# Moving a norm factor out of the linear operand of a gated feed-forward and giving its unit high and low activations in one 512-column matmul

## The chip, the cores and the metric

The kernel runs on one core of a Trainium2 chip. The metric is device time in microseconds (us) of the whole program, the median over executions. Inputs and outputs are float32.

## What is computed

Two transformer-like blocks on 256 tokens of width 1024: attention, feed-forward, a spatial gating unit, feed-forward again, then a state-space and attention mixer and an MLP. Every sub-block takes a normed input and its output is normed before it is added to the residual. The change touches the two feed-forwards:

```python
def rms_norm(x, g):
    y = xf * lax.rsqrt(jnp.mean(xf * xf, axis=-1, keepdims=True) + EPS)
    return y * g

def conv_gated_ffn(h, w_in, conv_w, conv_b, w_out):      # D_FF = 2816
    g, u = jnp.split(h @ w_in, 2, axis=-1)
    gp = jnp.pad(g, ((0, 0), (CONV_WIDTH - 1, 0), (0, 0)))
    g = conv_b + sum(conv_w[k] * gp[:, k:k + S] for k in range(CONV_WIDTH))
    return (jax.nn.gelu(g) * u) @ w_out

h = conv_gated_ffn(rms_norm(x, norm_ffn_pre[i]), ...)
x = x + rms_norm(h, norm_ffn_post[i])
```

Here g is the gated operand (it goes through the convolution and the gelu) and u is the linear one. The factor r of the norm in front belongs to a token, so it can be taken out of `h @ w_in`; u enters the output linearly, so r of u can be taken through `w_out` too, up to the following norm.

## The kernel before

All weights come in units of 128 x 1024 floats (512 KB) through a ring of six: SP loads `raw` (L2052), ScalarE rounds it to `w_hi` (`hi_of`, L151), VectorE computes the remainder `w_lo` (`lo_of`, L156). Activations are held as `a_hi` and `a_lo` in the same way, and a product of full precision is three matmuls, hi x hi, hi x lo and lo x hi (`three`, L172 to L175). A slot of the ring is free for rounding again when TensorE has used the unit (`unit_used`), and free for loading when `lo_done` says so.

**A feed-forward** has 22 tiles of 128 hidden features. For tile t TensorE runs (`ffn_in_pe`, L501) one unit for g and one for u, each `features` (L178): 8 slices of the width by three matmuls, with 256 moving columns (the tokens), 24 matmuls per unit. Two tiles behind, it runs `accumulate` (L205) for the output: 12 matmuls of 512 columns with one unit of `w_out` and the finished activations of tile t - 2. Tiles 0 to 3 are written out, tiles 4 to 19 are a hardware loop of two tiles per turn (`Fori`, with semaphore values and column addresses computed in registers), tiles 20 and 21 are written out again. The last four output units are held back (`held_pe`, L322) and run by token tile, first all four for token tile 0, then for token tile 1, so that the norm behind can begin. PSUM banks alternate by the parity of t (`f_banks`), so TensorE waits before the g unit of tile t until tile t - 2 has left its banks (L503).

Per tile **VectorE** runs, in its program's order (`ffn_dve_step`, L563): g times the row of norm factors `ROW` into `pad` (L572), the three taps of the convolution (L576, L580 twice), `w_lo` of two units ahead (the two calls of `split`), the product of gated and linear operand `F_PR` (L586), its remainder `a_lo` (L589), and a third `w_lo`. **ScalarE** (`ffn_act_step`, L534) runs: a `w_hi`, the gelu (L540), a `w_hi`, the rounding of `F_PR` to `a_hi` (L545), a `w_hi`. **GpSimd** (`ffn_pool_step`, L548) multiplies the gelu's result by `ROW` (L553). ScalarE waits for the convolution before the gelu and for `product` before the rounding; VectorE waits for `w_hi` before each `w_lo`, for GpSimd before the product and for `a_hi` before the remainder. What lies behind a waiting instruction of an engine waits with it.

**Between the sub-blocks** stands an `update` (L429 to L468): squares of the result for its norm (L368), the root (L376), the term `acc * row` (`term_dve`, L408), the reciprocal (L414), the addition to x (L418), transposition and rounding for the next sub-block, the factor of the next norm (L426). There are six updates; updates 1 and 3 follow the feed-forwards. `row_pe` and `row_dve` turn the factors of the norm before a feed-forward into `ROW` by two small matmuls and a copy.

Of the kernel before, what the change touches and what calls it, by code (L numbers as in the profile page):

```python
# [8 lines left out]
F32R = mybir.dt.float32r  # L9
# [77 lines left out]
def build(nc, w, x_in, cols_in, misc_in, tables_in, rows_in, ws_in, wdt_in, out):  # L87
    def sb(name, shape, dt=F32):
        return nc.alloc_sbuf_tensor(name, shape, dt)
# [11 lines left out]
    x = sb("x", [P, TT, D])  # L101


    a_hi = sb("a_hi", [P, 2 * KT, SEQ], F32R)
    a_lo = sb("a_lo", [P, 2 * KT, SEQ], F32R)
    cols = sb("cols", [P, COLS])
    misc = sb("misc", [P, MISC])
    tab = sb("tab", [P, TABLES])
# [69 lines left out]
    def features(pe, n, o, i=0, pre=None):  # L178
# [45 lines left out]

    Norm = namedtuple("Norm", "n sum mean root inv scaled turned hi lo")
    Pre = namedtuple("Pre", "lo base")
    Update = namedtuple("Update", "n n_last part base term sum root inv added next")

    ROW = cut(16384, SEQ)
    EPS_COL = st[:, 90:91]  # L230
# [70 lines left out]
                                     ALU.subtract).then_inc(q.lo, 1)  # L301


    def update(n, n_last):
        return Update(n, n_last, *post_sems, next_sems)

    acc = [ps[:, 2 * tt:2 * tt + 2, :].rearrange("p a b -> p (a b)") for tt in range(TT)]

# [62 lines left out]
    def root_act(act, u, tt):  # L371
        if tt:
            act.wait_ge(u.base, u.n + 1)
        act.wait_ge(u.sum, 3 * u.n + 2 * tt + 1)
        k = 23 if tt else 20
        act.activation(st[:, 4 + tt:5 + tt], st[:, k:k + 1], ACT.Sqrt, bias=st[:, 24:25] if tt else EPS_COL,  # L376
                       scale=1.0 / D).then_inc(u.root, 1)

    def next_act(act, u, tt):
        act.wait_ge(u.added, 4 * u.n + 2 * tt + 2)  # L380
# [19 lines left out]
    def term_dve(dve, u, tt, h, r):  # L400

        acc_ready(dve, u, tt, h)
        dve.wait_ge(u.sum, 3 * u.n + (h + 2 if tt else 1))
        if tt and h == 0:
            dve.tensor_scalar(st[:, 24:25], st[:, 22:23], 1.0 / D, EPS, ALU.mult, ALU.add).then_inc(u.base, 1)
        if tt == 0:
            dve.wait_ge(row_loaded[r % 2], 16 * (r // 2 + 1))
        dve.tensor_tensor(ybuf[:, tt, half(h)], acc[tt][:, half(h)], row[:, r % 2, half(h)],  # L408
                          ALU.mult).then_inc(u.term, 1)

    def add_dve(dve, u, tt):

# [8 lines left out]
    def half(h):  # L421
        return slice(h * D // 2, (h + 1) * D // 2)
# [60 lines left out]
            add_dve(dve, u, tt)  # L483


    F_CV, F_GL, F_PR, F_GR = cut(3072, 2, SEQ), cut(3584, 2, SEQ), cut(4096, 2, SEQ), cut(4608, 2, SEQ)

    def ffn_sems(name):
        return signals(name, "copied conv gelu scaled product hi lo")

    def f_g(n0, t):
        return n0 + (2 * t if t < 2 else 3 * t - 2 if t < FT - 1 else 3 * t - 3)
# [19 lines left out]
    def ffn_pe(pe, f, n0, u, following, turn_early=True):  # L512
        features(pe, n0, ps[:, 0, 0:SEQ], pre=after(u))
        row_pe(pe, u, 1)
        features(pe, n0 + 1, ps[:, 3, 0:SEQ])
        ffn_in_pe(pe, f, n0, 1)
        ffn_in_pe(pe, f, n0, 2)
        pe.wait_ge(next_sems.row_out, f_row[f])
        pe.wait_ge(f.lo, 1)
        accumulate(pe, f_out(n0, 0), f_slot(0), True, False)  # L520
        ffn_in_pe(pe, f, n0, 3)
        pe.wait_ge(f.lo, 2)
        accumulate(pe, f_out(n0, 1), f_slot(1), False, False)
# [31 lines left out]
    def ffn_pool(pool, f):  # L555
        pool.wait_ge(next_sems.row_out, f_row[f])
        for t in range(2):
            ffn_pool_step(pool, f, t)
        with pool.Fori(0, (FT - 2) // 2) as i:
            for t in (2, 3):  # L560
                ffn_pool_step(pool, f, t, i)
# [1479 lines left out]
    with nc.Block() as block:  # L2041
# [18 lines left out]
        def _(pool):  # L2060
# [71 lines left out]
        def _(dve):  # L2132
# [176 lines left out]
```

## Time and profile before

| | us |
|---|---|
| median of 3 runs | 1118.3 (1117.46 to 1119.08) |
| the profiled execution, device time | 1117.81 |
| its span, first to last instruction | 1116.0 |
| first feed-forward, first `pad` to last `a_lo` starting | 111.2 to 281.9 |
| second feed-forward, the same | 528.5 to 699.1 |

The profile names engines PE (TensorE matmul), PEld (its weight load), DVE (VectorE), ACT (ScalarE), POOL (GpSimd). Times of the timeline are from the start of the span. Matmuls are pipelined, so the distance from one start to the next is what one costs, not its own duration.

### The profile page before, as it was taken

What the parts mean: (1) busy time and instruction counts of PE and PEld (TensorE: products, weight loads), DVE (VectorE), ACT (ScalarE), POOL (GpSimd) and SP (SyncE); (2) the same over time, 40 slices, a digit from 0 to 9 for tenths busy, and PEclk for the clock granted to TensorE, in tenths of its full rate; (3) what the DMA queues carried; (4) which work ended last, traced back from release to release, by engine and by line L of the source; (5) the groups of instructions that cost most, each with busy time, mean ns of one, the idle gap of its engine ahead of it and who ended that gap; (6) DMA issues with size and microseconds to landing.
All of it is one profiled execution on the core that took longest, in us unless ns stands there. A gap on an engine that the chain in (4) does not pass through costs nothing.

```text
span 1116.0 us, 20509 instructions
## 1 busy us (share of the span) xinstructions
PE 1077.4 (97%) x7130; PEld 964.4 (86%) x7130; DVE 782.0 (70%) x1330; ACT 631.1 (57%) x1126; POOL 96.8 (9%) x119
## 2 busy tenths in 40 slices
PE   7989999999999999999999999999998998999998
PEld 7978999999788998788999999899576877999997
DVE  6657877777754457886877777798678748666664
ACT  6657444444755856666444444777767646444443
POOL 0140111111010002220111111000000000000000
PEclk9999999999999999999999999999999999999999
DMA  8353656555366374442655555364111544555541
GB/s 328 111 196 120 221 188 199 195 184 193 118 245 200 120 232 161 150 161 86 219 184 198 188 191 186 103 205 166 57 57 58 167 154 148 191 188 188 188 150 38
DMA packets 51381, 185.07 MB, mean 166 GB/s; under 512 B 5728, under 2 KB 6240, under 8 KB 51328
## 3 DMA queue, kind: packets, MB, share of 16 engines
q1 hardware_dynamic: 49248, 178.28, 48.2%
q0 software_dynamic: 1504, 5.44, 1.4%
q8 instruction: 34, 0.56, 0.2%
q10 hardware_dynamic: 576, 0.64, 0.2%
q14 instruction: 19, 0.16, 0.0%
HBM read 183.29 MB, written 1.05 MB: 165 GB/s over the span
## 4 chain that ended last, share of the span: by engine, by line
PE 88%; DVE 6%; ACT 3%; issue 2%; DMA 1%; DVEq 0%; SPq 0%; ACTq 0%
PE ps L215 28%; PE ps L173 18%; PE ps L175 18%; PE ps L174 18%; DVE w_lo L156 2%; PE ps L1559 1%; PE ps L675 1%; DVE a_lo L396 1%; ACT a_hi L390 1%; PE ps L704 1%; PE ps L688 1%; DVE arena L771 1%; PE ps L1570 1%; PE ps L939 1%; DMA x<-in_x 1%
## 5 line engine op out<-in xcount | busy, mean ns | idle before, releaser
L156 DVE TENSOR_TENSOR w_lo<-raw,w_hi 128x1024 fp32r<-128x1024 f32 x336 | 418.0, 1253 | 135.6 <-ACT w_hi L151 135.5
L151 ACT ACTIVATE w_hi<-raw 128x1024 fp32r<-128x1024 f32 x336 | 347.3, 1052 | 158.7 <-PE ps L175 100.1
L173 PE MATMUL ps<-a_hi,w_hi 128*128 128x256 f32 x1408 | 400.0, 284 | 2.2 <-DVE a_lo L396 1.4
L175 PE MATMUL ps<-a_hi,w_lo 128*128 128x256 f32 x1408 | 398.4, 283 | 0.0
L174 PE MATMUL ps<-a_lo,w_hi 128*128 128x256 f32 x1408 | 398.3, 283 | 0.0
L173 PEld LDWEIGHTS ps<-a_hi,w_hi 128*128 128x128 f32 x1408 | 269.8, 192 | 7.7 <-issue 3.6
L174 PEld LDWEIGHTS ps<-a_lo,w_hi 128*128 128x128 f32 x1408 | 269.9, 192 | 2.6
L175 PEld LDWEIGHTS ps<-a_hi,w_lo 128*128 128x128 f32 x1408 | 269.9, 192 | 0.0
L215 PE MATMUL ps<-w_hi,a_hi 128*128 128x512 f32 x496 | 162.4, 401 | 7.8 <-DVE a_lo L1144 2.8
L215 PE MATMUL ps<-w_lo,a_hi 128*128 128x512 f32 x496 | 157.7, 391 | 0.0
L215 PE MATMUL ps<-w_hi,a_lo 128*128 128x512 f32 x496 | 157.3, 390 | 0.0
L215 PEld LDWEIGHTS ps<-w_lo,a_hi 128*128 128x128 f32 x496 | 93.1, 188 | 20.5
L215 PEld LDWEIGHTS ps<-w_hi,a_lo 128*128 128x128 f32 x496 | 93.1, 188 | 20.5
L215 PEld LDWEIGHTS ps<-w_hi,a_hi 128*128 128x128 f32 x496 | 85.8, 189 | 23.8 <-issue 3.9
L540 ACT ACTIVATE arena<-arena 128x256 f32<-128x256 f32 x44 | 18.4, 418 | 101.4 <-DVE arena L580 101.4
L553 POOL TENSOR_TENSOR arena<-arena 128x256 f32<-128x256 f32 x44 | 47.1, 1071 | 309.8 <-ACT arena L540 309.8
L545 ACT ACTIVATE a_hi<-arena 128x256 fp32r<-128x256 f32 x44 | 18.4, 418 | 77.8 <-DVE arena L586 76.1
L173 PE MATMUL ps<-w_hi,a_hi 128*128 128x512 f32 (+1 forms) x160 | 61.2, 383 | 0.6 <-DVE a_lo L396 0.6
L175 PE MATMUL ps<-w_hi,a_lo 128*128 128x512 f32 (+1 forms) x160 | 59.0, 369 | 0.0
L174 PE MATMUL ps<-w_lo,a_hi 128*128 128x512 f32 (+1 forms) x160 | 59.0, 368 | 0.0
L580 DVE SCALAR_TENSOR_TENSOR arena<-pad,cols,arena 128x256 f32<-128x256 f32 x88 | 42.7, 485 | 10.2 <-DVE arena L576 0.3
L173 PEld LDWEIGHTS ps<-w_hi,a_hi 128*128 128x128 f32 x160 | 30.2, 188 | 7.7 <-issue 2.7
(193 smaller groups left out, 1007.9 us busy)
## 6 DMA issues: line engine op xcount, KB each, us to landing
raw<-in_w SPq DMA_DIRECT2D x336, 512.0 KB, 3.4
row<-in_rows POOLq DMA_DIRECT2D x7, 512.0 KB, 4.2
x<-in_x SPq DMA_DIRECT2D x2, 512.0 KB, 5.0
out<-x SPq DMA_DIRECT2D x4, 256.0 KB, 2.0
misc<-in_misc POOLq DMA_DIRECT2D x1, 512.0 KB, 5.6
arena<-in_ws POOLq DMA_DIRECT2D x1, 512.0 KB, 7.1
tab<-in_tables POOLq DMA_DIRECT2D x1, 320.0 KB, 4.4
tab<-in_tables POOLq DMA_DIRECT2D x1, 256.0 KB, 4.7
```

The costliest lines, as they stand in the source:

```text
L151: act.activation(w_hi[:, s, :], raw[:, s, :], ACT.Copy).then_inc(hi_done, 1)
L156: dve.tensor_tensor(w_lo[:, s, :], raw[:, s, :], w_hi[:, s, :].bitcast(F32), ALU.subtract).then_inc(lo_done, 1)
L173: pe.matmul(o, l_hi, r_hi, start=first, stop=False)
L174: pe.matmul(o, l_hi, r_lo, start=False, stop=False)
L175: return pe.matmul(o, l_lo, r_hi, start=False, stop=last)
L215: mm = pe.matmul(ps[:, 2 * tt + c, :], a[:, slot, t], b[:, s, c * 512:(c + 1) * 512], start=f, stop=z)
L390: act.activation(a_hi[:, k, tile(tt)], spun(tt, k), ACT.Copy, scale=gain(g, k)).then_inc(u.next.hi, 1)
L396: dve.scalar_tensor_tensor(a_lo[:, k, tile(tt)], spun(tt, k), gain(g, k), a_hi[:, k, tile(tt)].bitcast(F32), ALU.mult, ALU.subtract).then_ ...
L540: act.activation(F_GL[:, b, :], F_CV[:, b, :], ACT.Gelu_apprx_tanh).then_inc(f.gelu, 1)
L545: act.activation(a_hi[:, f_slot(t), :], F_PR[:, b, :], ACT.Copy).then_inc(f.hi, 1)
L553: pool.tensor_tensor(F_GR[:, b, :], F_GL[:, b, :], ROW, ALU.mult).then_inc(f.scaled, 1)
L580: dve.scalar_tensor_tensor(F_CV[:, b, :], pad[:, b, k:k + SEQ], col(k), F_CV[:, b, :], ALU.mult, ALU.add).then_inc(f.conv, 1)
```

## The change

The operand u is no longer multiplied by the norm factor. The product is gelu(g) times the unnormed u; the output of the feed-forward is then too large by 1/r per token, which updates 1 and 3 put right (`power` 1: the term is multiplied by r, and the mean of squares by r squared). GpSimd's product is gone. The u unit is computed by `features_apart`: `a_hi` and `a_lo` lie in one buffer `both`, and one matmul of 512 columns applies `w_hi` to both, with the results side by side in the bank; a second of 256 columns adds `w_lo` x `a_hi` to the first half. The halves must then be added: ScalarE copies the second half out of PSUM (`F_UP`), VectorE adds it to the first (`F_US`), and then multiplies. TensorE's wait at L503 is for the sum in place of the product. `factors_dve` (two operations of two columns each) stands on VectorE ahead of each feed-forward.

```diff
-    a_hi = sb("a_hi", [P, 2 * KT, SEQ], F32R)
-    a_lo = sb("a_lo", [P, 2 * KT, SEQ], F32R)
+    both = sb("both", [P, 2, 2 * KT, SEQ], F32R)
+    a_hi, a_lo = both[:, 0], both[:, 1]
...
+    def features_apart(pe, n, bank, i=0, pre=None):
+
+        s = n % RING
+        pe.wait_ge(lo_done, n + 1 + RING * i)
+        for k in range(KT):
+            if pre is not None:
+                pe.wait_ge(pre.lo, pre.base + k + 1)
+            c = slice(k * P, (k + 1) * P)
+            pe.matmul(ps[:, bank, :].rearrange("p (h t) -> p h t", h=2), w_hi[:, s, c], both[:, :, k, :],
+                      start=k == 0, stop=False)
+            mm = pe.matmul(ps[:, bank, 0:SEQ], w_lo[:, s, c], a_hi[:, k, :], start=False, stop=k == KT - 1)
+        mm.then_inc(unit_used, 1)
...
+    def factors_dve(dve, u):
+
+        n = sum(v.power > 0 for v in updates[:u.n])
+        dve.wait_ge(u.next.inv, TT * u.n)
+        r, f = st[:, 14:14 + TT], st[:, FACTOR:FACTOR + TT]
+        if u.power == 2:
+            dve.tensor_tensor(f, r, r, ALU.mult).then_inc(factor_ready, 1)
+        else:
+            dve.tensor_copy(f, r).then_inc(factor_ready, 1)
+        dve.wait_ge(factor_ready, 2 * n + 1)
+        dve.scalar_tensor_tensor(st[:, FACTOR_SQ:FACTOR_SQ + TT], f, 1.0 / D, f, ALU.mult,
+                                 ALU.mult).then_inc(factor_ready, 1)
...
-        dve.tensor_tensor(ybuf[:, tt, half(h)], acc[tt][:, half(h)], row[:, r % 2, half(h)],
-                          ALU.mult).then_inc(u.term, 1)
+        if u.power:
+            dve.scalar_tensor_tensor(ybuf[:, tt, half(h)], acc[tt][:, half(h)], factor(u, tt), row[:, r % 2, half(h)],
+                                     ALU.mult, ALU.mult).then_inc(u.term, 1)
...
     def ffn_in_pe(pe, f, n0, t, i=0):
         if t >= 3:
-            pe.wait_ge(f.product, t - 1 + 2 * i)
+            pe.wait_ge(f.summed, t - 1 + 2 * i)
         g_bank, u_bank = f_banks(t, i)
         features(pe, f_g(n0, t), ps[:, g_bank, 0:SEQ], i)
-        features(pe, f_g(n0, t) + 1, ps[:, u_bank, 0:SEQ], i)
+        features_apart(pe, f_g(n0, t) + 1, u_bank, i)
...
         act.wait_ge(f.conv, 3 * t + 3 + 6 * i)
         if t >= 2:
-            act.wait_ge(f.scaled, t - 1 + 2 * i)
+            act.wait_ge(f.product, t - 1 + 2 * i)
         act.activation(F_GL[:, b, :], F_CV[:, b, :], ACT.Gelu_apprx_tanh).then_inc(f.gelu, 1)
         split(1)
+        act.wait_ge(unit_used, f_g(n0, t) + 2 + RING * i)
+        if t >= 2:
+            act.wait_ge(f.summed, t - 1 + 2 * i)
+        act.activation(F_UP[:, b, :], ps[:, f_banks(t, i)[1], SEQ:2 * SEQ], ACT.Copy).then_inc(f.part, 1)
         act.wait_ge(f.product, t + 1 + 2 * i)
...
-    def ffn_pool_step(pool, f, t, i=0):
-        b = t % 2
-        pool.wait_ge(f.gelu, t + 1 + 2 * i)
-        if t >= 2:
-            pool.wait_ge(f.product, t - 1 + 2 * i)
-        pool.tensor_tensor(F_GR[:, b, :], F_GL[:, b, :], ROW, ALU.mult).then_inc(f.scaled, 1)
...
         split(0)
         split(1)
-        dve.wait_ge(f.scaled, t + 1 + 2 * i)
-        dve.wait_ge(unit_used, f_g(n0, t) + 2 + RING * i)
-        dve.tensor_tensor(F_PR[:, b, :], F_GR[:, b, :], ps[:, u_bank, 0:SEQ],
-                          ALU.mult).then_inc(f.product, 1)
+        dve.wait_ge(f.part, t + 1 + 2 * i)
+        dve.tensor_tensor(F_US[:, b, :], F_UP[:, b, :], ps[:, u_bank, 0:SEQ], ALU.add).then_inc(f.summed, 1)
+        dve.wait_ge(f.gelu, t + 1 + 2 * i)
+        dve.wait_ge(f.summed, t + 1 + 2 * i)
+        dve.tensor_tensor(F_PR[:, b, :], F_GL[:, b, :], F_US[:, b, :], ALU.mult).then_inc(f.product, 1)
...
+            factors_dve(dve, updates[1])
             ffn_dve(dve, ffn[0], N_FFN0, 0)
```

## Rows read from the trace of the kernel before

**Rows 1.** The page: the chain that ended last, shares of the span by engine.

```profile
PE 88%; DVE 6%; ACT 3%; issue 2%; DMA 1%; DVEq 0%; SPq 0%; ACTq 0%
```

**Rows 2.** Busy time in a stretch of the first feed-forward's loop (stretch, length, engines).

```profile
138.00:269.00 131.00, 131.00 (x925) 123.40 (x924) 97.78 (x145) 58.57 (x80) 16.73 (x16) 1.00 0.59 192
```

**Rows 3.** Timeline of PE over one tile: start, duration, instruction.

```profile
204.61 0.63 PE L215 MATMUL ps<-w_hi,a_hi 128*128 128x512 f32 x2
...
207.36 0.28 PE L173 MATMUL ps<-a_hi,w_hi 128*128 128x256 f32 x1
...
213.11 0.63 PE L215 MATMUL ps<-w_hi,a_hi 128*128 128x512 f32 x2
```

**Rows 4.** Timeline of DVE over the loop's tile t = 12.

```profile
204.00 0.42 DVE L572 TENSOR_TENSOR pad<-ps,arena 128x256 f32<-128x256 f32 x1
204.76 0.42 DVE L576 TENSOR_SCALAR arena<-pad,cols 128x256 f32<-128x256 f32 x1 [0.35 <-DVE pad L572]
...
207.96 1.30 DVE L156 TENSOR_TENSOR w_lo<-raw,w_hi 128x1024 fp32r<-128x1024 f32 x1 [0.38 <-ACT w_hi L151]
209.18 0.41 DVE L586 TENSOR_TENSOR arena<-arena,ps 128x256 f32<-128x256 f32 x1
210.15 0.42 DVE L589 TENSOR_TENSOR a_lo<-arena,a_hi 128x256 fp32r<-128x256 f32 x1 [0.56 <-ACT a_hi L545]
211.10 1.23 DVE L156 TENSOR_TENSOR w_lo<-raw,w_hi 128x1024 fp32r<-128x1024 f32 x1 [0.53 <-ACT w_hi L151]
212.25 0.42 DVE L572 TENSOR_TENSOR pad<-ps,arena 128x256 f32<-128x256 f32 x1
```

**Rows 5.** Timeline of ACT over the same tile.

```profile
206.88 1.05 ACT L151 ACTIVATE w_hi<-raw 128x1024 fp32r<-128x1024 f32 x1
...
209.70 0.42 ACT L545 ACTIVATE a_hi<-arena 128x256 fp32r<-128x256 f32 x1 [1.78 <-DVE arena L586]
```

**Rows 6.** Timeline of DVE: `pad` of tiles 4 and 19.

```profile
138.27 0.42 DVE L572 TENSOR_TENSOR pad<-ps,arena 128x256 f32<-128x256 f32 x1
...
261.50 0.42 DVE L572 TENSOR_TENSOR pad<-ps,arena 128x256 f32<-128x256 f32 x1
```

**Rows 7.** Timeline of DVE in the last two tiles, 20 and 21.

```profile
269.93 0.42 DVE L572 TENSOR_TENSOR pad<-ps,arena 128x256 f32<-128x256 f32 x1 [0.17 <-PE ps L175]
...
273.96 1.23 DVE L156 TENSOR_TENSOR w_lo<-raw,w_hi 128x1024 fp32r<-128x1024 f32 x1 [0.98 <-ACT w_hi L151]
...
281.89 0.43 DVE L589 TENSOR_TENSOR a_lo<-arena,a_hi 128x256 fp32r<-128x256 f32 x1 [0.48 <-ACT a_hi L545]
```

**Rows 8.** Timeline of PE: first matmul of tile 21, first of the last held unit.

```profile
272.61 0.28 PE L173 MATMUL ps<-a_hi,w_hi 128*128 128x256 f32 x1
...
282.48 0.63 PE L215 MATMUL ps<-w_hi,a_hi 128*128 128x512 f32 x2
```

**Rows 9.** Timeline of DVE in the first tiles, written out.

```profile
111.22 0.42 DVE L572 TENSOR_TENSOR pad<-ps,arena 128x256 f32<-128x256 f32 x1
111.67 0.41 DVE L576 TENSOR_SCALAR arena<-pad,cols 128x256 f32<-128x256 f32 x1
...
114.56 1.38 DVE L156 TENSOR_TENSOR w_lo<-raw,w_hi 128x1024 fp32r<-128x1024 f32 x1 [0.30 <-ACT w_hi L151]
115.87 0.41 DVE L586 TENSOR_TENSOR arena<-arena,ps 128x256 f32<-128x256 f32 x1
```

**Rows 10.** Groups of instructions on DVE (busy us, mean ns).

```profile
L418 DVE SCALAR_TENSOR_TENSOR x<-arena,st,x 128x512 f32<-128x512 f32 x24 | 17.0, 749 | 0.4
L408 DVE TENSOR_TENSOR arena<-ps,row 128x512 f32<-128x512 f32 x24 | 15.9, 683 | 20.9 <-ACT arena L368 16.2 <-issue 4.6
L414 DVE RECIPROCAL st<-st 128x1 f32<-128x1 f32 x12 | 1.8, 152 | 0.0
```

**Rows 11.** Timeline of PE, and its busy time with granted clock, behind a long wait.

```profile
855.99 1.54 PE L675 MATMUL ps<-arena 64*128 64x256 f32 x6 [2.68 <-DVE stq L771]
...
856.00:860.00 4.00, 4.00 (x20) 0.57 0.00 0
```

More of the change, by code:

```diff
@@ L226, in build @@
     Pre = namedtuple("Pre", "lo base")
-    Update = namedtuple("Update", "n n_last part base term sum root inv added next")
+    Update = namedtuple("Update", "n n_last power part base term sum root inv added next")
     ROW = cut(16384, SEQ)
@@ L301, in halves_dve, with update, factor, mean_scale @@
                                      ALU.subtract).then_inc(q.lo, 1)
-    def update(n, n_last):
-        return Update(n, n_last, *post_sems, next_sems)
+    def update(n, n_last, power):
+        return Update(n, n_last, power, *post_sems, next_sems)
+    factor_ready = sem("factor_ready")
+    FACTOR, FACTOR_SQ = 40, 44
+    def factor(u, tt):
+        return st[:, FACTOR + tt:FACTOR + tt + 1]
+    def mean_scale(u, tt):
+        return st[:, FACTOR_SQ + tt:FACTOR_SQ + tt + 1] if u.power else 1.0 / D
+    def factors_dve(dve, u):
[9 more added lines that the diff above has]
+                                 ALU.mult).then_inc(factor_ready, 1)
+    def factors_there(eng, u):
+        if u.power:
+            eng.wait_ge(factor_ready, 2 * sum(v.power > 0 for v in updates[:u.n + 1]))
     acc = [ps[:, 2 * tt:2 * tt + 2, :].rearrange("p a b -> p (a b)") for tt in range(TT)]
@@ L375, in root_act @@
         k = 23 if tt else 20
+        factors_there(act, u)
         act.activation(st[:, 4 + tt:5 + tt], st[:, k:k + 1], ACT.Sqrt, bias=st[:, 24:25] if tt else EPS_COL,
-                       scale=1.0 / D).then_inc(u.root, 1)
+                       scale=mean_scale(u, tt)).then_inc(u.root, 1)
     def next_act(act, u, tt):
@@ L403, in term_dve @@
         dve.wait_ge(u.sum, 3 * u.n + (h + 2 if tt else 1))
+        factors_there(dve, u)
         if tt and h == 0:
-            dve.tensor_scalar(st[:, 24:25], st[:, 22:23], 1.0 / D, EPS, ALU.mult, ALU.add).then_inc(u.base, 1)
+            dve.tensor_scalar(st[:, 24:25], st[:, 22:23], mean_scale(u, tt), EPS, ALU.mult,
+                              ALU.add).then_inc(u.base, 1)
         if tt == 0:
             dve.wait_ge(row_loaded[r % 2], 16 * (r // 2 + 1))
-        dve.tensor_tensor(ybuf[:, tt, half(h)], acc[tt][:, half(h)], row[:, r % 2, half(h)],
-                          ALU.mult).then_inc(u.term, 1)
+        if u.power:
+            dve.scalar_tensor_tensor(ybuf[:, tt, half(h)], acc[tt][:, half(h)], factor(u, tt), row[:, r % 2, half(h)],
+                                     ALU.mult, ALU.mult).then_inc(u.term, 1)
+        else:
+            dve.tensor_tensor(ybuf[:, tt, half(h)], acc[tt][:, half(h)], row[:, r % 2, half(h)],
+                              ALU.mult).then_inc(u.term, 1)
     def add_dve(dve, u, tt):
@@ L483, in last_update_dve @@
             add_dve(dve, u, tt)
-    F_CV, F_GL, F_PR, F_GR = cut(3072, 2, SEQ), cut(3584, 2, SEQ), cut(4096, 2, SEQ), cut(4608, 2, SEQ)
+    F_CV, F_GL, F_PR = cut(3072, 2, SEQ), cut(3584, 2, SEQ), cut(4096, 2, SEQ)
+    F_UP, F_US = cut(4608, 2, SEQ), cut(5120, 2, SEQ)
     def ffn_sems(name):
-        return signals(name, "copied conv gelu scaled product hi lo")
+        return signals(name, "copied conv gelu part summed product hi lo")
     def f_g(n0, t):
@@ L514, in ffn_pe @@
         row_pe(pe, u, 1)
-        features(pe, n0 + 1, ps[:, 3, 0:SEQ])
+        features_apart(pe, n0 + 1, 3)
         ffn_in_pe(pe, f, n0, 1)
@@ L546, in ffn_act_step @@
         split(2)
-    def ffn_pool_step(pool, f, t, i=0):
-        b = t % 2
-        pool.wait_ge(f.gelu, t + 1 + 2 * i)
-        if t >= 2:
-            pool.wait_ge(f.product, t - 1 + 2 * i)
-        pool.tensor_tensor(F_GR[:, b, :], F_GL[:, b, :], ROW, ALU.mult).then_inc(f.scaled, 1)
[L555 to L561, printed above, removed]
     def ffn_dve_step(dve, f, n0, layer, t, i, split):
@@ L2034, in build @@
     first, mix = Norm(0, *pre_sems), Norm(1, *pre_sems)
-    updates = [update(n, begins - 1) for n, begins in enumerate((N_FFN0, N_SGV, N_FFN1, N_MIX, N_MLP, UNITS))]
+    updates = [update(n, begins - 1, power)
+               for n, (begins, power) in enumerate(((N_FFN0, 0), (N_SGV, 1), (N_FFN1, 0), (N_MIX, 1), (N_MLP, 0), (UNITS, 0)))]
     ffn = [ffn_sems("ffn0"), ffn_sems("ffn1")]
@@ L2085, in _ @@
             load_row(3)
-            ffn_pool(pool, ffn[0])
             updated(1)
@@ L2091, in _ @@
             load_row(5)
-            ffn_pool(pool, ffn[1])
             updated(3)
@@ L2147, in _ @@
             update_dve(dve, updates[2], 3, 3, False, 3)
+            factors_dve(dve, updates[3])
             ffn_dve(dve, ffn[1], N_FFN1, 1)
```

## The prediction

> **What bounds the kernel now.** The page comes first: the chain that ended last is TensorE for 88% of the span [rows 1]. The busy times of a stretch of the loop say the same, TensorE 131 of 131 us, VectorE 98, ScalarE 59, GpSimd 17 [rows 2]. So a reader may take VectorE and ScalarE to have 25% to spare. The timelines of one tile say otherwise, and there I read on.
>
> TensorE: the 12 matmuls of 512 columns take 207.36 - 204.61 = 2.75 us, 229 ns each; the 48 of 256 columns take 213.11 - 207.36 = 5.75, 120 ns each. A tile is 8.50 us [rows 3].
>
> VectorE: from `pad` of tile 12 to `pad` of tile 13 it is 8.25 us [rows 4]; over tiles 4 to 19 it is (261.50 - 138.27) / 15 = 8.215 [rows 6]. No wait in this tile is for TensorE: those shown are 0.35 for `pad`, 0.38, 0.56 and 0.53 for ScalarE [rows 4], and ScalarE waits in turn for VectorE's product before it rounds [rows 5]. It is one serial chain that changes engines: convolution, gelu and `w_hi`, `w_lo`, product, `a_hi`, `w_hi`, `w_lo`, next `pad`. It is long because each engine waits for the other. It begins behind TensorE and gains 8.50 - 8.215 = 0.285 us per tile, so that it meets TensorE at tile 20 (0.17 us of waiting) [rows 7]. **The room is 0.285 us per tile, and 0.20 if TensorE becomes faster by what the change saves.**
>
> The end has none. The last remainder `a_lo` starts at 281.89, ends at 282.32 [rows 7], and TensorE starts the last held unit that needs it at 282.48 [rows 8].
>
> **Part by part, for one feed-forward.**
>
> TensorE. A u unit goes from 24 x 120 ns to 8 x (229 + 120): 2.880 to 2.792, 0.09 us less per tile, 22 tiles, 1.9 us. Bounds for the 512-column pass over two separate pieces of SBUF, which no row shows: 213 ns would be an even share of nothing but columns (229 less the 16 that are over), 240 is two passes of 256. I take 229, the rows' own. A page sees it differently: the Trainium skill, TensorE: Matmul & The Clock Gate, section "Wait — 56ns, not 53.3ns?", puts the fixed cost of a warm matmul at about 2.5 ns; by that, as an estimate, eight matmuls fewer save 0.02 us per tile, 0.4 us in all, where the rows' 2 x 120 - 229 = 11 ns give 1.9. In either case the saving counts only where TensorE bounds.
>
> GpSimd's product goes. It is beside VectorE's second `w_lo`, which takes 115.87 - 114.56 = 1.31 in the written-out tiles [rows 9] and 209.18 - 207.96 = 1.22 in the loop, against 212.25 - 211.10 = 1.15 for the third `w_lo`, which has no GpSimd beside it [rows 4]. Gain on the chain: 0.16 written out, 0.07 in the loop. The product of VectorE waited for nothing before (it starts as `w_lo` ends), so no wait goes away.
>
> ScalarE's `F_UP`, 256 columns, some 0.42 as its other operations of that width [rows 5]. It follows the `w_hi` that ends at 207.93 [rows 5], while VectorE is at a `w_lo` until 209.18 [rows 4]: covered, up to a price of 1.25. u itself has been in PSUM for over 3 us at that point. ScalarE's rounding waits for the product anyway.
>
> VectorE's `F_US`: 0.41, as the product it resembles [rows 4], and the product then waits for it. That wait is 0.03 in written-out tiles (111.22 + 0.42 to 111.67) [rows 9] and at most 0.35 in the loop, where values for several waits and columns are computed in between [rows 4]; the product has no register column and its one other wait is passed beforehand, so I take 0.03. **This addition lies on the serial chain**, behind it `a_hi`, `a_lo` and the next `w_hi`. Net: 0.44 - 0.07 = +0.37 in the loop, 0.44 - 0.16 = +0.28 written out. Ends: +0.27 in the loop (an addition that overlaps its neighbours, 0.34, less 0.07) and +0.55 (0.41 + 0.14 of waiting, no gain from GpSimd).
>
> `factors_dve` ahead of tile 0: two operations of 0.15 [rows 10], the second behind the first: +0.25 (0.15 to 0.35). VectorE's `pad` follows its `w_lo` at once there.
>
> In the loop the chain is now 8.215 + 0.37 = 8.585 and TensorE 8.41: they change places. TensorE, ahead so far, isn't stopped at once; the bank's wait (L503) catches it at tile 21. It would be there at 272.61 [rows 8] - 20 x 0.09 = 270.8. `pad` of tile 19 moves from 261.50 by 0.25 + 4 x 0.28 + 15 x 0.37 = 6.9 to 268.4, its sum is ready 5.5 later, at 273.9: a stop of some 3 us. The tile behind is no loss, since the chain is later still.
>
> The end: last `a_lo` later by 0.25 + 4 x 0.28 + 16 x 0.37 + 0.44 (tile 20, where a wait already kept `w_lo` clear of GpSimd) + 0.31 (tile 21) = 8.0, less what VectorE now waits through TensorE in tile 20, 0.17 and 0.98 - 0.33 = 0.65 [rows 7]: **+7.2 us**. It ends at 289.5. TensorE finishes u of tile 21 at 273.9 + 5.7 = 279.6, two held units at 282.3, the third (its `a_lo` is there at 283.4) at 284.7: it then stands still for 4.8 us, where it had stood for 0.2.
>
> The clock. Behind a wait of 2.68 us the granted clock has a mean of 0.57 over 4 us [rows 11], one stretch at 1.2 GHz in place of 2.4 between full-speed ones. That cost 0.43 x 4 = 1.7 us of matmul work. After 4.8 us I expect the same, now on the path, as the held units that follow are the chain: +1.7 (0 to 3.4, if two such stretches fall there).
>
> The update behind: four terms become three-operand operations, 0.749 in place of 0.683 [rows 10], some two of them on the path: +0.1.
>
> Sum: 7.2 + 1.7 + 0.1 = 9.0 per feed-forward. The second has the same timing: first `pad` to last `a_lo` within 0.1 us of the first's by the table. So +18.0 on the profiled execution's 1117.8 (span 1116.0 and 1.8 around it), 1135.8; the median stands 0.5 above that execution, hence **1136**.
>
> **The rivals.**
>
> Clock kept: the chain grows, but TensorE's stop causes no slow stretch. 7.3 x 2: 1132.9. Against it is the one wait of comparable length. 0.19.
>
> A dearer chain: the loop pays register time before the product and gains nothing from GpSimd, +0.55 x 16 + 0.45 x 6 + 0.35 - 0.82 = 11.0, with clock and update 12.8 each: 1144. 0.12.
>
> TensorE still bounds (faster): if the sum and its wait add less than 0.20 us to the chain, for example hidden in the 0.35 to 0.56 that VectorE idles at each wait, TensorE is never stopped in the loop. VectorE has tile 20's g at 269.74 - 1.8 and needs 12.4 + 0.75 - 0.65 from there, so the last `a_lo` is 1.7 earlier, in both 3.4: 1114.6. For it: 25% of VectorE idle. Against it: the idle is ScalarE's work on the same chain, so an operation between two waits lengthens it by all of itself. Below 0.2 would need an addition at half the price of every row of its size. 0.06. About no change, from a mixture near that point: 0.03.
>
> The change doesn't save on TensorE, or loses: the wide pass costs more than two narrow ones. Below 250 ns this changes nothing, as the chain is longer; at 300 ns a tile is 8.98 us, 22 x 0.48 = 10.6 each: 1139. 0.04. The forecast: 0.56.
>
> **How the numbers follow.** 1136 is the likeliest case. Its own bounds: +0.27 per loop tile, cheap factors and no slow stretch give 4.9 per feed-forward, 1128; the dearer chain gives 1144. The faster case alone is left outside on that side: range 1128 to 1144. A measurement of this kernel tells 0.2% (2.2 us) from no change. Faster 0.06, within 0.2% 0.03, slower 0.91.
>
> **What would show it.** Right: `pad` to `pad` near 8.6 us in the loop, the new addition and product 0.44 apart; a `w_lo` of 1.22 everywhere; TensorE waiting for the sum at tile 21 by some 3 us and for the last `a_lo` by 4 to 5; the granted clock at half once or twice there; u units of 2.79 us. Wrong: a `pad` distance of 8.4, with TensorE solid through the loop, means that the serial chain had more room than I read; a rise of the update's time by microseconds, or a later start of tile 0, means that I placed the cost in the wrong stage.

## The result, and the profile after

The changed kernel takes 1139.6 us in the median of six runs (1137.9 to 1141.2), the kernel before 1117.9 beside it: a ratio of 1.0196, 95% interval 1.0186 to 1.0206. The forecast was 1136, with a range of 1128 to 1144. The profiled execution took 1139.09 us; its span is 1137.3, which is 21.3 longer than before.

The same stretch of the loop as in [rows 2], from the changed kernel (stretch, length, busy time of PE, PEld, DVE, ACT, POOL, granted clock, DMA):

```profile
138.00:269.00 131.00, 130.99 (x801) 116.38 (x800) 97.94 (x152) 59.51 (x91) 0.00 (x0) 1.00 0.56 183
```

The busy times don't show the loss: VectorE is as busy as before, GpSimd not at all, TensorE is full. Even the number of matmuls, 801 in place of 925, is lower through the wide pass, which makes 52 matmuls of a tile's 60. TensorE runs ahead of the serial chain through most of this stretch; where it is caught is shown below.

The timeline of VectorE over the loop's tile 12, to lay beside [rows 4]:

```profile
210.71 0.42 DVE L608 TENSOR_TENSOR pad<-ps,arena 128x256 f32<-128x256 f32 x1
211.48 0.41 DVE L612 TENSOR_SCALAR arena<-pad,cols 128x256 f32<-128x256 f32 x1 [0.35 <-DVE pad L608]
...
214.67 1.23 DVE L156 TENSOR_TENSOR w_lo<-raw,w_hi 128x1024 fp32r<-128x1024 f32 x1 [0.38 <-ACT w_hi L151]
215.81 0.41 DVE L621 TENSOR_TENSOR arena<-arena,ps 128x256 f32<-128x256 f32 x1
216.33 0.43 DVE L624 TENSOR_TENSOR arena<-arena 128x256 f32<-128x256 f32 x1
217.32 0.42 DVE L626 TENSOR_TENSOR both<-arena,both 128x256 fp32r<-128x256 f32 x1 [0.56 <-ACT both L596]
218.27 1.23 DVE L156 TENSOR_TENSOR w_lo<-raw,w_hi 128x1024 fp32r<-128x1024 f32 x1 [0.53 <-ACT w_hi L151]
219.42 0.42 DVE L608 TENSOR_TENSOR pad<-ps,arena 128x256 f32<-128x256 f32 x1
```

`pad` to `pad` is 8.71 here. Every wait for ScalarE is what it was, 0.38, 0.56 and 0.53. The chain of the two engines goes through the same steps, and the addition (L621) is one step more. The second `w_lo` takes 215.81 - 214.67 = 1.14 in place of 1.22. ScalarE over the same tile, beside [rows 5]:

```profile
213.59 1.05 ACT L151 ACTIVATE w_hi<-raw 128x1024 fp32r<-128x1024 f32 x1
214.54 0.37 ACT L592 ACTIVATE arena<-ps 128x256 f32<-128x256 f32 x1
216.87 0.42 ACT L596 ACTIVATE both<-arena 128x256 fp32r<-128x256 f32 x1 [1.96 <-DVE arena L624]
```

The copy out of PSUM (L592) ends at 214.91, 0.9 us before the addition reads it: it is covered. Next come the two operations of `factors_dve` ahead of tile 0, `pad` of tiles 4 and 19 (beside [rows 6]), and the last `a_lo` of each feed-forward (beside [rows 7]):

```profile
112.48 0.17 DVE L337 COPY st<-st 128x2 f32<-128x2 f32 x1
112.68 0.16 DVE L339 SCALAR_TENSOR_TENSOR st<-st 128x2 f32<-128x2 f32 x1
112.76 0.42 DVE L608 TENSOR_TENSOR pad<-ps,arena 128x256 f32<-128x256 f32 x1
...
141.31 0.42 DVE L608 TENSOR_TENSOR pad<-ps,arena 128x256 f32<-128x256 f32 x1
...
271.41 0.42 DVE L608 TENSOR_TENSOR pad<-ps,arena 128x256 f32<-128x256 f32 x1
...
292.20 0.42 DVE L626 TENSOR_TENSOR both<-arena,both 128x256 fp32r<-128x256 f32 x1 [0.48 <-ACT both L596]
...
720.19 0.43 DVE L626 TENSOR_TENSOR both<-arena,both 128x256 fp32r<-128x256 f32 x1 [0.48 <-ACT both L596]
```

(271.41 - 141.31) / 15 = **8.673 us per tile, 8.215 before.** From first `pad` to last `a_lo` it is 179.44, 170.67 before: 8.77 more. The factors ahead of the first `pad` add 0.28.

TensorE, one tile of the loop and its two stops in each feed-forward, beside [rows 3] and [rows 8]:

```profile
202.85 0.40 PE L198 MATMUL ps<-both,w_hi 128*128 128x512 f32 x1
203.09 0.28 PE L200 MATMUL ps<-both,w_lo 128*128 128x256 f32 x1
203.20 0.40 PE L198 MATMUL ps<-both,w_hi 128*128 128x512 f32 x1
...
205.68 0.62 PE L228 MATMUL ps<-w_hi,both 128*128 128x512 f32 x2
...
214.12 0.40 PE L228 MATMUL ps<-w_hi,both 128*128 128x512 f32 x1
...
276.90 0.58 PE L173 MATMUL ps<-both,w_hi 128*128 128x256 f32 x1 [2.66 <-DVE arena L621]
...
292.68 0.50 PE L228 MATMUL ps<-w_hi,both 128*128 128x512 f32 x1 [4.44 <-DVE both L626]
...
704.90 0.38 PE L173 MATMUL ps<-both,w_hi 128*128 128x256 f32 x1 [2.66 <-DVE arena L621]
...
720.67 0.80 PE L228 MATMUL ps<-w_hi,both 128*128 128x512 f32 x1 [4.59 <-DVE both L626]
```

A tile in which TensorE isn't stopped is 214.12 - 205.68 = 8.44; the u unit is 205.68 - 202.85 = 2.83. The wait for the bank (L503 of the kernel before) catches TensorE well ahead of tile 21: at tile 17, whose g unit may start when the sum of tile 15 is there. These are that sum and the first matmul of the unit:

```profile
241.78 0.41 DVE L621 TENSOR_TENSOR arena<-arena,ps 128x256 f32<-128x256 f32 x1
...
242.33 0.38 PE L173 MATMUL ps<-both,w_hi 128*128 128x256 f32 x1
```

The sum ends at 242.19, and TensorE starts 0.14 behind it. From there on it keeps the pace of the chain: the g units of tiles 17 to 21 start at 242.33, 251.03, 259.66, 268.28 and 276.90, 8.64 apart in the mean. The 2.66 us of waiting at tile 21 are what the 12 matmuls of an output unit (2.75) fill in the tiles ahead; behind tile 20 there are none, as they are held back. For the last `a_lo` TensorE waits 4.44 and 4.59. The clock behind these two stops (same columns as the first fence):

```profile
293.00:297.00 4.00, 4.00 (x12) 3.15 (x11) 0.81 (x2) 1.97 (x4) 0.00 (x0) 0.57 0.30 120
720.00:724.00 4.00, 3.33 (x9) 2.69 (x10) 0.43 (x1) 1.80 (x3) 0.00 (x0) 0.57 0.45 151
```

A mean of 0.57 each, as in [rows 11]: one stretch at 1.2 GHz in each.

So the 21.3 us of the span are made up as follows. Up to the last `a_lo` it is 2 x 9.05. From its end to the next mark outside the feed-forward it is 1.67 and 1.39: after the first, to the start of TensorE's wait of 1.0 us in a later update, 231.92 us before and 233.59 now; after the second, to the start of a wait of 0.7 us in the mixer, 22.65 and 24.04. The remaining 0.1 has nothing to do with the change. This execution has a slow stretch in the attention near 61 us that the one of before hasn't (1.47, less 0.2 for an earlier start, +1.26 together), and near 856 us it is the other way round (-1.17).

### The profile page after: what moved, and what is told of

The parts are those of the page before. It is cut to its first block and busy times, and to the rows that moved or that the text cites. A ratio compares the mean times of both kernels' runs of the same rounds, so it can differ in the third digit from the quotient of the medians.

```text
span 1137.3 us, 19775 instructions
## 1 busy us (share of the span) xinstructions
PE 1082.8 (95%) x6778; PEld 948.4 (83%) x6778; DVE 798.0 (70%) x1378; ACT 642.5 (56%) x1170; POOL 49.7 (4%) x75
## 5 line engine op out<-in xcount | busy, mean ns | idle before, releaser
L228 PE MATMUL ps<-w_hi,both 128*128 128x512 f32 x992 | 296.4, 398 | 17.7 <-DVE both L626 9.9
L173 PE MATMUL ps<-both,w_hi 128*128 128x256 f32 x1056 | 302.5, 286 | 8.3 <-DVE arena L621 6.0
L174 PE MATMUL ps<-both,w_hi 128*128 128x256 f32 x1056 | 299.4, 283 | 0.0
L175 PE MATMUL ps<-both,w_lo 128*128 128x256 f32 x1056 | 299.4, 283 | 0.0
L228 PEld LDWEIGHTS ps<-w_hi,both 128*128 128x128 f32 x992 | 180.4, 190 | 57.1 <-DVE both L626 11.1
L173 PEld LDWEIGHTS ps<-both,w_hi 128*128 128x128 f32 x1056 | 203.0, 192 | 18.5 <-DVE arena L621 8.3
L174 PEld LDWEIGHTS ps<-both,w_hi 128*128 128x128 f32 x1056 | 203.1, 192 | 2.2
L175 PEld LDWEIGHTS ps<-both,w_lo 128*128 128x128 f32 x1056 | 202.9, 192 | 0.0
L228 PE MATMUL ps<-w_lo,both 128*128 128x512 f32 x496 | 158.5, 393 | 0.0
L198 PE MATMUL ps<-both,w_hi 128*128 128x512 f32 x352 | 126.5, 399 | 0.0
L228 PEld LDWEIGHTS ps<-w_lo,both 128*128 128x128 f32 x496 | 93.9, 189 | 20.7
L200 PE MATMUL ps<-both,w_lo 128*128 128x256 f32 x352 | 99.0, 281 | 0.0
L198 PEld LDWEIGHTS ps<-both,w_hi 128*128 128x128 f32 x352 | 66.3, 188 | 14.1
L200 PEld LDWEIGHTS ps<-both,w_lo 128*128 128x128 f32 x352 | 66.6, 189 | 0.0
L173 PE MATMUL ps<-w_hi,both 128*128 128x512 f32 (+1 forms) x160 | 61.2, 382 | 0.6 <-DVE both L436 0.6
L175 PE MATMUL ps<-w_hi,both 128*128 128x512 f32 (+1 forms) x160 | 59.0, 369 | 0.0
```

Source lines behind the costliest of these rows:

```text
L173: pe.matmul(o, l_hi, r_hi, start=first, stop=False)
L174: pe.matmul(o, l_hi, r_lo, start=False, stop=False)
L175: return pe.matmul(o, l_lo, r_hi, start=False, stop=last)
L198: pe.matmul(ps[:, bank, :].rearrange("p (h t) -> p h t", h=2), w_hi[:, s, c], both[:, :, k, :], start=k == 0, stop=False)
L200: mm = pe.matmul(ps[:, bank, 0:SEQ], w_lo[:, s, c], a_hi[:, k, :], start=False, stop=k == KT - 1)
L228: mm = pe.matmul(ps[:, 2 * tt + c, :], a[:, slot, t], b[:, s, c * 512:(c + 1) * 512], start=f, stop=z)
```

## The experiments

**The addition alone.** Is it the addition on the serial chain, or something else of the change?

```diff
...
         dve.wait_ge(unit_used, f_g(n0, t) + 2 + RING * i)
+        dve.tensor_tensor(F_EX[:, b, :], F_GL[:, b, :], ps[:, u_bank, 0:SEQ], ALU.add).then_inc(f.extra, 1)
+        dve.wait_ge(f.extra, t + 1 + 2 * i)
         dve.tensor_tensor(F_PR[:, b, :], F_GR[:, b, :], ps[:, u_bank, 0:SEQ],
                           ALU.mult).then_inc(f.product, 1)
```

> The kernel before with one more 256-column VectorE operation ahead of the product (a sum of the gelu's result and the bank of u into a buffer that nobody reads), and the product waiting for it; no wide pass, GpSimd's product still there. Serial chain theory: pad to pad in the loop goes from 8.215 to 8.7 us, the last a_lo of each feed-forward comes some 10 us later, TensorE stops there and its clock falls once on the path: 1139 to 1142 us. If the wide pass, the split buffer or the operations in the update were what costs, this stays at 1118 us.

Measured: 1139.9 us, ratio 1.0204 (1.0187 to 1.0221). VectorE and TensorE of this kernel:

```profile
213.33 1.30 DVE L156 TENSOR_TENSOR w_lo<-raw,w_hi 128x1024 fp32r<-128x1024 f32 x1 [0.38 <-ACT w_hi L151]
214.55 0.41 DVE L587 TENSOR_TENSOR arena<-arena,ps 128x256 f32<-128x256 f32 x1
215.00 0.42 DVE L589 TENSOR_TENSOR arena<-arena,ps 128x256 f32<-128x256 f32 x1
...
291.49 1.22 PE L215 MATMUL ps<-w_hi,a_hi 128*128 128x512 f32 x2 [3.80 <-DVE a_lo L592]
```

One operation of 0.41 us, 0.45 with its wait, makes the whole slowdown with no other part of the change, stop of TensorE included. From first `pad` to last `a_lo` it is 179.93, and a loop tile is 8.675 in the mean. That this is so close to the 8.673 of the changed kernel is chance: there 0.08 is saved at the second `w_lo` and about as much lost elsewhere (the experiment with the wait moved shows where).

**The change without the addition.** ScalarE still copies, but the product reads the first half of the bank, so that this kernel leaves out one part of u.

```diff
...
-        dve.tensor_tensor(F_US[:, b, :], F_UP[:, b, :], ps[:, u_bank, 0:SEQ], ALU.add).then_inc(f.summed, 1)
         dve.wait_ge(f.gelu, t + 1 + 2 * i)
-        dve.wait_ge(f.summed, t + 1 + 2 * i)
-        dve.tensor_tensor(F_PR[:, b, :], F_GL[:, b, :], F_US[:, b, :], ALU.mult).then_inc(f.product, 1)
+        dve.tensor_tensor(F_PR[:, b, :], F_GL[:, b, :], ps[:, u_bank, 0:SEQ], ALU.mult).then_inc(f.product, 1)
```

> The changed kernel without the addition: the product reads the first half of the bank directly, so the high-by-low part of u is left out of the result (ScalarE still copies it). Serial chain theory: the chain is 8.215 - 0.07 + 0.02 = 8.17 us per tile, under TensorE's 8.43, which bounds again; per feed-forward 22 x 0.067 us less on TensorE, 0.2 us for the factors: 1115 to 1116.5 us, no stop of TensorE over 0.5 us in the feed-forward. If the wide pass or the update costs, it stays near 1139 us.

Measured: 1115.7 us, ratio 0.9988 (0.9978 to 0.9998). The long stops are gone, and a loop tile of the chain is 8.158 in the mean. All the other parts of the change together cost nothing and gain a little.

**The change without the wide pass.** u as before, in 24 narrow matmuls; no copy, no addition; the norm factor is moved and GpSimd's product gone.

```diff
-        features_apart(pe, f_g(n0, t) + 1, u_bank, i)
+        features(pe, f_g(n0, t) + 1, ps[:, u_bank, 0:SEQ], i)
...
-        dve.wait_ge(f.part, t + 1 + 2 * i)
-        dve.tensor_tensor(F_US[:, b, :], F_UP[:, b, :], ps[:, u_bank, 0:SEQ], ALU.add).then_inc(f.summed, 1)
+        dve.wait_ge(unit_used, f_g(n0, t) + 2 + RING * i)
```

> The changed kernel with u computed as before (24 matmuls of 256 columns, all three parts into one half), no copy and no addition: only the norm factor is moved and GpSimd's product is gone. Serial chain theory: chain 8.17, TensorE 8.50 per tile, TensorE bounds; factors and update cost 0.2 to 0.5 us per feed-forward, tile 21 gives 0.1 back: 1117.5 to 1118.5 us. Against e2_no_sum it prices the wide pass: 44 x 0.067 = 2.9 us slower than that.

Measured: 1117.4 us, ratio 1.0005 (0.9994 to 1.0015). Taking a multiplication from GpSimd is worth nothing here, as TensorE bounds with 8.50 us per tile. The ratios of this kernel and the one without the addition differ by 0.0017, or 1.9 us, which is the gain of the wide pass; 2.9 were expected, and the intervals allow it.

**Another order.** The same operations, copy and addition where the engines stand idle, first ScalarE's order and then VectorE's:

```diff
         split(0)
+        act.wait_ge(unit_used, f_g(n0, t) + 2 + RING * i)
+        if t >= 2:
+            act.wait_ge(f.summed, t - 1 + 2 * i)
+        act.activation(F_UP[:, b, :], ps[:, f_banks(t, i)[1], SEQ:2 * SEQ], ACT.Copy).then_inc(f.part, 1)
         act.wait_ge(f.conv, 3 * t + 3 + 6 * i)
...
         split(0)
-        split(1)
         dve.wait_ge(f.part, t + 1 + 2 * i)
         dve.tensor_tensor(F_US[:, b, :], F_UP[:, b, :], ps[:, u_bank, 0:SEQ], ALU.add).then_inc(f.summed, 1)
+        split(1)
         dve.wait_ge(f.gelu, t + 1 + 2 * i)
```

> The changed kernel with the same operations in another order: ScalarE's copy ahead of the gelu, where it idles 2.7 us per tile, and VectorE's addition between its two w_lo, where it idles 0.38 us for w_hi. Serial chain theory: the chain is 8.2 to 8.3 us per tile, TensorE bounds with 8.43, and the kernel comes to 1115 to 1118 us (the last two tiles may pay for the copy's wait for u). If the amount of work on VectorE counts and not its place, it stays at 1135 to 1140 us.

Measured: 1115.7 us, ratio 0.9980 (0.9970 to 0.9991). Timed a second time:

> The same kernel as e3_sum_early, timed again beside the kernel before: 0.998 of it, 1115 to 1116 us.

Measured: 1115.8 us, ratio 0.9977 (0.9968 to 0.9986). VectorE of the first, one tile:

```profile
202.80 0.42 DVE L608 TENSOR_TENSOR pad<-ps,arena 128x256 f32<-128x256 f32 x1
...
205.16 1.22 DVE L156 TENSOR_TENSOR w_lo<-raw,w_hi 128x1024 fp32r<-128x1024 f32 x1
206.29 0.41 DVE L620 TENSOR_TENSOR arena<-arena,ps 128x256 f32<-128x256 f32 x1
206.68 1.23 DVE L156 TENSOR_TENSOR w_lo<-raw,w_hi 128x1024 fp32r<-128x1024 f32 x1
207.82 0.42 DVE L624 TENSOR_TENSOR arena<-arena 128x256 f32<-128x256 f32 x1
...
210.90 0.42 DVE L608 TENSOR_TENSOR pad<-ps,arena 128x256 f32<-128x256 f32 x1
```

This tile's chain is 8.10 us with the addition in it, and 8.176 in the mean of the loop, against 8.158 without any addition: in this place the addition costs 0.02 us and not 0.45. It fills the 0.38 that VectorE otherwise waits for `w_hi`. In the stretch from 138 to 269 us VectorE is busy for 102.0 us, 4 more than in the changed kernel, and the program is 24 us faster. This settles place against amount.

**The clock.** Small matmuls where TensorE stands still, into a bank that is free then:

```diff
+        pe.wait_ge(f.copied, FT - 2)
+        for _ in range(14):
+            pe.matmul(ps[:, 5, SEQ:SEQ + P], ident, ident, start=True, stop=True)
         ffn_in_pe(pe, f, n0, FT - 1)
...
+            if k == HELD - 1:
+                for _ in range(28):
+                    pe.matmul(ps[:, 4, SEQ:SEQ + P], ident, ident, start=True, stop=True)
             pe.wait_ge(f.lo, FT - HELD + k + 1)
```

> The changed kernel with 14 small matmuls into a bank not in use ahead of tile 21 and 28 ahead of the last held unit, where TensorE stands still for 2.7 and 4.4 us. If the slow stretch behind the stop lies on the path with 1.4 to 1.7 us per feed-forward, this gives 1136 to 1137 us and a granted clock of 1.00 there. If the clock is hidden behind the other engines it stays at 1139.6 us.

Measured: 1139.0 us, ratio 1.0189 (1.0170 to 1.0208), with no slow stretch behind the stops of the feed-forwards. By itself this would have spoken for a clock that is hidden behind other engines; the timeline of TensorE shows another reason:

```profile
288.32 6.41 PE L587 MATMUL ps<-tab 128*128 128x128 f32 x56
294.49 0.70 PE L228 MATMUL ps<-w_hi,both 128*128 128x512 f32 x2
```

The 28 small matmuls (two records each in the trace) ran for 6.2 us, and the held unit began at 294.49, though its `a_lo` had ended at 293.0. The small matmuls ate what the clock gave back. So the run was repeated with 11 and 18 of them:

> As e4_warm with 11 and 18 small matmuls in place of 14 and 28: in e4_warm the 28 took 6.1 us, and TensorE came to the last held unit 1.5 us after its operand. If the slow stretch costs 1.4 to 1.7 us per feed-forward on the path, this gives 1136 to 1137 us. If the clock is hidden, it stays at 1139.6 us.

Measured: 1135.8 us, ratio 1.0160 (1.0146 to 1.0174). From last `a_lo` to the first `pad` of the second feed-forward it is 1.65 us less than in the changed kernel, and from the second feed-forward's last `a_lo` to the wait in the mixer 1.35 less. So the slow stretch is on the path, with 3.0 us in all; the median falls by 3.8. (The profiled execution happened to have no slow stretch near 61 us either, which is worth 1.47 us of its own time.) The same two distances bound what the operations in the update cost: less 0.28 for the factors in the first, they are within 0.05 us of those of the kernel before.

```profile
286.39 4.18 PE L587 MATMUL ps<-tab 128*128 128x128 f32 x36
291.15 0.73 PE L228 MATMUL ps<-w_hi,both 128*128 128x512 f32 x2 [0.58 <-DVE both L637]
...
290.00:294.00 4.00, 3.42 (x18) 2.74 (x17) 0.61 (x2) 2.83 (x5) 0.00 (x0) 1.00 0.58 179
```

**One wait moved.** In the changed kernel the product comes 216.33 - (215.81 + 0.41) = 0.11 us behind the addition's end (0.10 in the mean), where 0.03 were forecast.

```diff
+        dve.wait_ge(f.gelu, t + 1 + 2 * i)
         dve.wait_ge(f.part, t + 1 + 2 * i)
         dve.tensor_tensor(F_US[:, b, :], F_UP[:, b, :], ps[:, u_bank, 0:SEQ], ALU.add).then_inc(f.summed, 1)
-        dve.wait_ge(f.gelu, t + 1 + 2 * i)
```

> The changed kernel with the wait for the gelu ahead of the addition, so that the product has one wait instead of two. Serial chain theory: from the addition's end to the product 0.10 us become 0.03 to 0.04, pad to pad 8.67 becomes 8.61 in the loop, 22 x 0.065 = 1.4 us per feed-forward: 1136.5 to 1137 us. If the gap of 0.10 us is an operand's price (the product reads SBUF twice) and not the second wait's, it stays.

Measured: 1136.7 us, ratio 1.0163 (1.0144 to 1.0183), in five runs from 1134.1 to 1139.6.

```profile
214.95 0.42 DVE L622 TENSOR_TENSOR arena<-arena,ps 128x256 f32<-128x256 f32 x1
215.40 0.42 DVE L624 TENSOR_TENSOR arena<-arena 128x256 f32<-128x256 f32 x1
...
292.00:296.00 4.00, 4.00 (x11) 3.07 (x11) 0.73 (x2) 1.50 (x3) 0.00 (x0) 0.50 0.21 85
```

The gap is 0.03. The second wait of an instruction costs 0.07 us here, although what it waits for had come long ago. A loop tile is 8.601 in place of 8.673, and from first `pad` to last `a_lo` it is 1.59 us less in each feed-forward, 3.2 in all. The median says much the same, 2.9, but it alone would be weak evidence, for the runs spread by more. The last row shows why: the granted clock is 0.50 over the whole of 292 to 296 us. In this profiled execution (1138.95 us) two slow stretches come one behind the other at each long stop, the first beginning while TensorE still stands, where the profiled execution of the changed kernel has one. The distances behind the last `a_lo` are longer by 1.0 us in each feed-forward for it.

**The tail.** In tile 21 the two units rounded between belong to the next sub-block. Here they come behind the remainder:

```diff
-        for t in range(FT - 2, FT):
-            step(t, 0, lambda j, t=t: half_to(eng, f_g(n0, t) + 6 + min(j, 1)))
+        step(FT - 2, 0, lambda j: half_to(eng, f_g(n0, FT - 2) + 6 + min(j, 1)))
+        step(FT - 1, 0, lambda j: half_to(eng, f_g(n0, FT - 1) + 7) if j == 2 else None)
```

> The changed kernel with the rounding of the two ring units in tile 21 (both belong to the next sub-block) behind the tile's own remainder. Serial chain theory: the last a_lo comes 2.5 to 2.8 us earlier in each feed-forward, TensorE's stop at the last held unit shrinks from 4.4 to about 2 us: 1134 to 1135 us, less if the slow stretch goes too. If the end of the feed-forward were TensorE's, it stays at 1139.6 us.

Measured: 1135.1 us, ratio 1.0151 (1.0137 to 1.0165). TensorE's stop at the last held unit is 2.38 us in the first feed-forward and 2.78 in the second, where the changed kernel has 4.44 and 4.59. A slow stretch still follows the stop of 2.38 (mean clock 0.58 from 290 to 294 us), but none follows that of 2.78 (1.00 from 716 to 720). From first `pad` to last `a_lo` it is 1.9 less and not 2.5 to 2.8, as the addition now waits 0.76 for ScalarE's copy, which the `w_lo` had covered:

```profile
287.69 0.42 DVE L621 TENSOR_TENSOR arena<-arena,ps 128x256 f32<-128x256 f32 x1 [0.76 <-ACT arena L592]
...
289.61 0.73 PE L228 MATMUL ps<-w_hi,both 128*128 128x512 f32 x2 [2.38 <-DVE both L626]
```

The same edit on top of the other order, where TensorE bounds:

> e3_sum_early with tile 21's ring units behind the remainder too. There TensorE waits 0.18 us for the last a_lo and no more, so the serial chain theory gives 0.2 us per feed-forward at most: 1115 to 1116 us, not to be told from e3_sum_early. If the chain still counted, it would gain up to 2 us per feed-forward.

Measured: 1114.8 us, ratio 0.9967 (0.9955 to 0.9979); the interval overlaps that of the other order alone (0.9968 to 0.9986). The two can't be told apart, as expected, and each is a little faster than the kernel before (0.2 to 0.3%) and clearly faster than the changed one.

**GpSimd beside VectorE.** The changed kernel with GpSimd's product put back, into a buffer that nobody reads:

```diff
             act.wait_ge(f.product, t - 1 + 2 * i)
+            act.wait_ge(f.scaled, t - 1 + 2 * i)
...
+        pool.tensor_tensor(F_GR[:, b, :], F_GL[:, b, :], ROW, ALU.mult).then_inc(f.scaled, 1)
...
```

> The changed kernel with GpSimd's product put back beside it, into a buffer that nobody reads (ScalarE's gelu waits for it two tiles later). If GpSimd beside VectorE's second w_lo costs what the rows of before show, that w_lo takes 1.22 in the loop and 1.30 in written-out tiles in place of 1.14: 4 x 0.16 + 16 x 0.08 + 0.3 = 2.2 us per feed-forward on the chain, 1143 to 1145 us. If those differences were something else's, it stays at 1139.6 us.

Measured: 1143.7 us, ratio 1.0231 (1.0216 to 1.0246). A written-out tile and a loop tile:

```profile
115.17 1.38 DVE L156 TENSOR_TENSOR w_lo<-raw,w_hi 128x1024 fp32r<-128x1024 f32 x1 [0.30 <-ACT w_hi L151]
116.47 0.41 DVE L639 TENSOR_TENSOR arena<-arena,ps 128x256 f32<-128x256 f32 x1
...
215.00 1.24 DVE L156 TENSOR_TENSOR w_lo<-raw,w_hi 128x1024 fp32r<-128x1024 f32 x1 [0.44 <-ACT w_hi L151]
216.17 0.41 DVE L639 TENSOR_TENSOR arena<-arena,ps 128x256 f32<-128x256 f32 x1
```

Where the tiles are written out, the `w_lo` takes 1.30 again in place of 1.14, all of it GpSimd. In the loop the time came out as expected for a wrong reason: `w_lo` takes 1.17, 0.03 more, and it begins 0.06 later, 0.44 behind for 0.38. That delay is ScalarE's: its gelu has one wait more in this kernel and starts 0.17 us behind the convolution, 0.12 in the changed kernel. So the 4.2 us are not all GpSimd's. The price goes with how long GpSimd's product still runs when the `w_lo` starts, by the trace's rough times for GpSimd: 0.29 to 0.31 us where 0.16 is lost, 0.21 in the loop of the kernel before (0.08 lost) and 0.17 here (0.03 lost).

The Trainium skill, SBUF — State Buffer, section "Who interferes with whom", says that a VectorE instruction with two SBUF inputs contends with a GpSimd one that reads SBUF, and calls the shared ports an exclusive lock. That there is contention agrees (1.30 against 1.14); whether one engine stands entirely for as long as the other holds the ports can't be read from these records.

## Why the prediction was right

**The bound.** Right. TensorE was full before, and the serial chain of VectorE and ScalarE had 0.285 us per tile to spare in spite of 25% idle time. One operation of 0.41 us on it gave the whole slowdown in the kernel before; without it, or with it in VectorE's idle time, the kernel is a little faster than before (0.1 to 0.2%). The faster rival's argument, that waits hide an operation, holds only for an operation placed in the wait, and there it holds but for 0.02 us. (That rival's time was also added up wrongly: 269.74 - 1.8 + 12.4 + 0.75 - 0.65 is 1.45 us ahead of the last `a_lo` of [rows 7], not 1.7. It changes nothing in the choice.)

**The addition's cost, mis-sized.** The step "I take 0.03" for the product's wait failed. It was 0.10, since the product had two waits, of which the earlier passed at once; I had taken that as free. With that wait moved the gap was 0.03, and the chain 3.2 us shorter in all. The product itself, with both inputs in SBUF, took 0.426 against 0.407. Together 0.09 a tile: the loop gained 0.458 and not 0.37, written-out tiles 0.37 and not 0.28 (6.26 for 5.89), 22 x 0.09 = 2.0 us. So the last `a_lo` came 9.05 later, where the sum said 7.2. Over two feed-forwards that is 3.7 us. The forecast was short by 3.6 in the median and by 3.3 in the profiled execution, since the part behind the last `a_lo` (1.67 and 1.39 for 2 x 1.8) gave 0.5 back.

**The factors and GpSimd.** The factors were put at 0.25 and measured 0.28. GpSimd's share of 0.16 in written-out tiles was confirmed by putting it back. For the loop, 0.07 was the difference between 1.22 and 1.15; the changed kernel shows 0.08. With GpSimd put back it was 0.03 only, at a later start of the `w_lo` relative to GpSimd's product.

**TensorE.** The u unit was to take 2.79 and took 2.83 in the tile shown, 2.81 by the tile's 8.433 over the loop. The wide pass is between the even 229 ns and the two narrow ones, at 231 to 236. The saving is 0.067 per tile, not 0.09. The prediction's estimate from the 2.5 ns of the Trainium skill, TensorE: Matmul & The Clock Gate, section "Wait — 56ns, not 53.3ns?", was 0.02 per tile, a third of what was measured, so here the rows were the better guide. The saving didn't count until the chain was shortened, and is then about 2 us (1.9 by the ratios; 2.9 by 44 x 0.067).

**The stops.** The wait at tile 21 was put at "some 3" us and is 2.66, but that is luck in part. The prediction had TensorE run ahead up to tile 21 and arrive at 270.8; it is held at the chain's pace from tile 17 on. It arrives at 276.90 - 2.66 = 274.24, less the 1.26 by which this execution is late before the feed-forward begins: 272.98, which is 2.2 later. The sum it waits for came 1.7 later than forecast (276.84 - 1.26 = 275.6 for 273.9), and the two errors nearly cancel. The time doesn't depend on it, as the chain sets the pace either way. At the last held unit it is 4.44 and 4.59 for 4.8.

**The clock.** The slow stretch was put at 1.7 us, with 0 to 3.4 as bounds, and is 1.65 and 1.35 on the path in the two profiled executions compared. The rival without it is refuted: the clock did fall, and filling the stop with the right number of small matmuls gave the time back. That it was one stretch and not two was luck of the execution. With two in a row, as in the kernel with the wait moved, the same part costs about 1.0 us more per feed-forward. The two longest of the changed kernel's six runs, 1140.7 and 1141.2 us, have mean clocks of 0.989 and 0.986 where the profiled one has 0.994; whether two stretches in a row are the reason there isn't shown.

**The update.** A term takes 0.744 us in place of 0.683 in updates 1 and 3. It was not tried by itself; on the path it is at most 0.05 us per feed-forward by the run with 11 and 18 small matmuls, where 0.1 was forecast. In the kernel with narrow matmuls factors and terms together don't show in the total.

## What to carry to other kernels

An idle share of an engine isn't room. If its waits are for an engine that waits for it in turn, measure the distance from one tile's start to the next and compare it with the bounding engine's. An operation that goes between two waits of such a chain costs all of itself (0.45 us here); put into a wait it costs almost nothing (0.02). And when work is taken from a third engine, ask first whether anybody waited for it.

## What the runs showed of the hardware

A second wait on a VectorE instruction costs 0.07 us on the chain even when it has long been fulfilled (product 0.10 behind the addition, 0.03 with one wait); put ahead of the addition, which begins as a `w_lo` ends, it costs nothing.

18 float32 matmuls of 128 x 128 take 4.18 us, 0.23 each, so filling a stop needs counting in both directions: 28 of them ate the gain. A matmul of 512 columns whose moving operand lies in two pieces takes 0.231 to 0.236 us against 0.229 for one piece.

Slow stretches of the clock fall, or don't, in the same place of the same program from run to run: near 61 us, worth 1.47 us, and near 856, worth 1.17. After equal stops of 2.66 us at tile 21 the changed kernel has one in the first feed-forward (mean clock 0.57 from 276 to 280 us) and none in the second (1.00 from 704 to 708). At the stops of 3.8 to 4.7 us that were not filled, every profiled execution has at least one, and some have two in a row (the kernel with the wait moved, at both; the one with the addition alone, at the first; the one with GpSimd's product back, at the second).
